# Nineteen gathered expert rows moved into the projections of tiles 1 to 3, in a layer kernel with product-key retrieval

## The chip, the cores and the metric

One Trainium2 chip, one of its cores. The metric is the device time of one execution in microseconds; the number given for a kernel is the median over its runs.

## What is computed

One layer over 512 positions (4 tiles of 128) and 2048 channels: a normed input projection, attention and a gated mix, an output projection added to `x`, and then the part that matters here, a retrieval of experts. Each position chooses 8 x 16 of 16384 experts by its query; each expert is one row of `peer_u` and one row of `peer_v` (2048 float32 numbers, 8 KB).

```python
def block(args):
    hb, idx, gb = args
    u_sel = jnp.take(expert_u, idx, axis=0)
    act = jax.nn.gelu(jnp.einsum('tkd,td->tk', u_sel, hb).astype(jnp.float32), approximate=False) * gb
    v_sel = jnp.take(expert_v, idx, axis=0)
    return jnp.einsum('tk,tkd->td', act.astype(hb.dtype), v_sel)
```

## The kernel before

**Two ways to the same sum.** For 304 of the positions of tiles 1 to 3 the kernel computes all experts densely on TensorE (PE): weights stream through a ring in pieces of 1 MB (128 x 2048 float32). For tile 0 (128 positions) and the last 80 positions it gathers the chosen rows: one "row" is an indirect DMA that brings one expert row to each of 128 partitions, so again 1 MB. VectorE (DVE) takes each row of `peer_u` times the normed input and sums it (line 1461, "u" rows), ScalarE (ACT) takes the GELU, and DVE adds each row of `peer_v`, weighted, to an accumulator of four PSUM banks called `acc` (lines 1472 and 1474, "v" rows). There are 128 u and 128 v rows for tile 0, then `out` (adds x and stores tile 0), `h` (loads the input of the last positions), 64 + 16 u rows and 64 + 16 v rows: 419 entries in `ROWS`, always in that order, each tied by `ROWS_AT` (line 121) to a piece during whose turn DVE takes it.

**A piece.** `load_upto` (line 480, the sync queue SP) loads piece n once PE has freed its place. ACT writes the high half `ring_hi` (`hi_upto`, line 735, instruction at 744); DVE (`lo_upto`, line 1180, instruction at 1188) or GpSimd (POOL, `make_lo`, line 655, instruction at 658) writes the low half `ring_lo`; PE waits for the low half and multiplies. The ring has three slots in the output projection of tiles 1 to 3 (pieces 112 to 127, `OUT_B`, PE line 1847) and the query projection (128 to 143, `QUERY_B`, PE line 2130), and four from piece 144 (`AHEAD`) on.

**The stages.** Pieces 112 to 127 run from 749 us, 128 to 143 from 897 us, the up stage with retrieval from 1048 us (pieces 144 to 215, PE lines 2145 to 2147), the down stage (216 to 283) from about 1600 us, and the last stage, up and down in turn (284 to 395), from about 2060 to 2840 us. In all but a few pieces of the projections DVE makes the low halves.

**The order of the work on DVE.** In the output projection DVE's loop (line 1591) makes for piece n the low halves up to n + 1, adds x after every fourth piece (`add_x1`), makes the low halves up to n + 2 (line 1597), and takes the rows of n. In the query projection (line 1614) it makes the low halves up to n + 2 (line 1617) and then takes the rows. From line 1626 it finishes the query sums, copies `h_far` (tile 0's normed input) into `acc` (line 1637), so that the place of `h_far` becomes row buffer 3, and begins the retrieval of tiles 1 to 3.

**The order of the work on POOL.** POOL issues the gathers in the order of `ROWS` (`gather`, line 677, the DMA at 695 or 703), each when the row that last used its buffer has been taken (`row_used`). In the projections it has nothing else to do. From piece 144 on it makes the low half of n and then issues the gathers whose buffers should be free (`gather_freed_before`, line 671). The first row in buffer 3 (`H_ROW`) waits for the copy of `h_far` (line 691). After `out` its buffer's next gather first stores tile 0 and waits for that store (lines 684 and 685).

**Row buffers.** 8 KB a partition each. `row_buffers` (line 175) takes of those allowed at a row's position the one free longest: 0 and 1 always, 4 up to piece 104, 2 from piece 112, 3 from piece 144. So the projections have three.

## Time and profile before

| what | us |
|---|---|
| median of 3 runs (least, most) | 2888.29 (2881.99, 2889.8) |
| the profiled execution, by itself | 2884.2 |
| its span, first to last instruction | 2882.5 |
| PE busy in the span | 2769.8 |
| granted TensorE clock, mean | 0.986 |

The profile is of one execution. Busy time of PE is modelled for the end of a matmul, so matmul counts per stretch are read beside it. "DMA share" is the mean busy share of the core's 16 DMA engines, and GB/s what they moved.

### The profile page before, as it was taken

The page shows a single profiled execution, that of the slowest core. Times are in us where ns is not written, and L with a number is a line of the kernel's source. Part 1 is how long each engine was busy: PE and PEld are TensorE (multiplying, and loading weights), DVE is VectorE, ACT ScalarE, POOL GpSimd, SP SyncE. Part 2 cuts the span into 40 slices and gives each one's busy share as a digit, 9 for nine tenths or more (in the row PEclk, how much of TensorE's full clock was granted, in tenths as well). Part 3 has the DMA queues.
Part 4 walks back from the last instruction along what each step waited for, and adds up shares of the span by engine and source line. Part 5 has one row for each costly group of instructions (what it writes and reads, how often), then busy time and mean ns, then how long its engine had stood idle before and what let it go on. Part 6 is the DMA issues. An engine that isn't in the chain of part 4 may idle for free.

```text
span 2882.5 us, 43296 instructions
## 1 busy us (share of the span) xinstructions
PE 2769.8 (96%) x17757; PEld 2612.8 (91%) x17757; DVE 2156.8 (75%) x2920; ACT 1256.1 (44%) x1692; POOL 1485.8 (52%) x657
## 2 busy tenths in 40 slices
PE   8899999988999999999999999998999999999998
PEld 6687778866788999999999999998999999999998
DVE  6856897767587778889997677776676777777786
ACT  7656632347424333337775333333333333333332
POOL 0100253322232348872223788887867776767762
PEclk9999999999999999999999999999999999999999
DMA  9747678974697969998999999999999999999996
GB/s 362 297 154 273 242 265 344 341 268 156 252 347 289 359 255 338 339 347 346 361 363 372 379 367 382 375 373 336 359 370 358 385 363 378 377 384 361 384 344 229
DMA packets 188846, 949.47 MB, mean 329 GB/s; under 512 B 17712, under 2 KB 77152, under 8 KB 78912
## 3 DMA queue, kind: packets, MB, share of 16 engines
q1 hardware_dynamic: 116064, 485.54, 45.1%
q0 software_dynamic: 60848, 440.59, 39.2%
q10 hardware_dynamic: 11808, 21.70, 2.1%
q8 instruction: 74, 1.21, 0.2%
q14 instruction: 52, 0.43, 0.0%
HBM read 906.46 MB, written 41.22 MB: 329 GB/s over the span
## 4 chain that ended last, share of the span: by engine, by line
PE 73%; DMA 9%; DVE 9%; ACT 5%; POOL 2%; issue 2%; SPq 0%; ACTq 0%; DVEq 0%; POOLq 0%
PE ps L1847 9%; PE ps L2147 9%; PE ps L2145 9%; PE ps L2146 9%; PE ps L2214 8%; PE ps L2216 8%; PE ps L2215 8%; PE ps L2130 5%; PE ps L1834 3%; DVE ring_lo L1188 3%; DMA rows<-peer_u_rows,idx_far 2%; PE ps L2188 2%; DMA g_in<-gelu_scratch 2%; POOL ring_lo L658 2%; DVE rows L1461 2%; ACT ring_hi L744 2%
## 5 line engine op out<-in xcount | busy, mean ns | idle before, releaser
L658 POOL TENSOR_TENSOR ring_lo<-ring_raw,ring_hi 128x2048 fp32r<-128x2048 f32 x203 | 942.2, 4642 | 527.7 <-ACT ring_hi L744 525.6
L744 ACT ACTIVATE ring_hi<-ring_raw 128x2048 fp32r<-128x2048 f32 x396 | 754.7, 1917 | 664.8 <-DMA ring_raw<-peer_u 233.5
L2214 PE MATMUL ps<-a_hi,ring_hi 128*128 128x304 f32 x2048 | 624.0, 305 | 19.9 <-POOL ring_lo L658 13.8
L2145 PE MATMUL ps<-bT_hi,ring_hi 128*128 128x304 f32 x2048 | 622.7, 304 | 9.8 <-POOL ring_lo L658 8.3
L2216 PE MATMUL ps<-a_hi,ring_lo 128*128 128x304 f32 x2048 | 620.0, 303 | 0.0
L2147 PE MATMUL ps<-bT_hi,ring_lo 128*128 128x304 f32 x2048 | 617.8, 302 | 0.0
L2215 PE MATMUL ps<-a_lo,ring_hi 128*128 128x304 f32 x2048 | 617.0, 301 | 0.0
L2146 PE MATMUL ps<-bT_lo,ring_hi 128*128 128x304 f32 x2048 | 615.7, 301 | 0.0
L1188 DVE TENSOR_TENSOR ring_lo<-ring_raw,ring_hi 128x2048 fp32r<-128x2048 f32 x197 | 460.6, 2355 | 129.8 <-ACT ring_hi L744 129.5
L695 POOL DMA_INDIRECT rows<-peer_u_rows,idx_far x128 | 206.0, 1609 | 452.8 <-DVE z_far L1461 398.0
L2214 PEld LDWEIGHTS ps<-a_hi,ring_hi 128*128 128x128 f32 x2048 | 386.2, 189 | 25.2 <-issue 17.9
L2145 PEld LDWEIGHTS ps<-bT_hi,ring_hi 128*128 128x128 f32 x2048 | 386.6, 189 | 10.9 <-issue 5.2
L2215 PEld LDWEIGHTS ps<-a_lo,ring_hi 128*128 128x128 f32 x2048 | 387.3, 189 | 0.5 <-issue 0.5
L2216 PEld LDWEIGHTS ps<-a_hi,ring_lo 128*128 128x128 f32 x2048 | 386.7, 189 | 0.0
L2146 PEld LDWEIGHTS ps<-bT_lo,ring_hi 128*128 128x128 f32 x2048 | 386.7, 189 | 0.0
L2147 PEld LDWEIGHTS ps<-bT_hi,ring_lo 128*128 128x128 f32 x2048 | 386.5, 189 | 0.0
L1736 DVE TENSOR_TENSOR yT<-ps,yT 128x304 f32<-128x304 f32 x496 | 222.1, 469 | 142.5 <-PE ps L2216 127.5
L1474 DVE SCALAR_TENSOR_TENSOR ps<-rows,a_far,ps 128x2048 f32<-128x2048 f32 x127 | 298.4, 2350 | 35.9 <-DMA rows<-peer_v_rows,idx_far 27.9
L1461 DVE CUSTOM_DVE_ANT_0 rows<-rows,h_far 128x2048 f32<-128x2048 f32 x116 | 280.7, 2436 | 52.3 <-DMA rows<-peer_u_rows,idx_far 52.1
L695 POOL DMA_INDIRECT rows<-peer_v_rows,idx_far x128 | 150.0, 1172 | 206.4 <-DVE ps L1474 191.1
L1461 DVE CUSTOM_DVE_ANT_0 rows<-rows,ps 128x2048 f32<-128x2048 f32 x92 | 208.9, 2280 | 20.6 <-DMA rows<-peer_u_rows,chosen 11.3
L1847 PE MATMUL ps<-ring_hi,bT_hi 128*128 128x512 f32 x660 | 187.6, 393 | 9.7 <-DVE ring_lo L1188 9.0
(328 smaller groups left out, 3759.8 us busy)
## 6 DMA issues: line engine op xcount, KB each, us to landing
ring_raw<-peer_u SPq DMA_DIRECT2D x128, 1024.0 KB
ring_raw<-peer_v SPq DMA_DIRECT2D x128, 1024.0 KB
...
```

The costliest lines, as they stand in the source:

```text
L658: pool.tensor_tensor(ring_lo[s][:], ring_raw[s][:], ring_hi[s][:].bitcast(F32), ALU.subtract)\
L695: pool.indirect_dma_start(out=dst[:], out_offset=None, in_=u_rows if kind == "u" else v_rows, in_offset=bass.IndirectOffsetOnAxis(ap=idx_f ...
L744: act.activation(ring_hi[place(n)][:], ring_raw[place(n)][:], ACT.Copy).then_inc(hi_ok[SLOT[n]], 1)
L1188: dve.tensor_tensor(ring_lo[s][:], ring_raw[s][:], ring_hi[s][:].bitcast(F32), ALU.subtract)\
L1461: dve.tensor_tensor_reduce(out=src, in0=src, in1=h_far[:] if r < FIRST_PSUM_ROW else acc, scale=1.0, scalar=0.0, op0=ALU.mult, op1=ALU.add ...
L1847: last = pe.matmul(ps[:, bank + t, :], w[:, k, t * P:(t + 1) * P], m[s][:, cols], start=first, stop=end)
L2145: pe.matmul(dst, hi[:, e], bT_hi[:, k, 0:NEAR], start=(k == 0), stop=False)
L2146: pe.matmul(dst, hi[:, e], bT_lo[:, k, 0:NEAR], start=False, stop=False)
L2147: last = pe.matmul(dst, lo[:, e], bT_hi[:, k, 0:NEAR], start=False, stop=(k == KD - 1))
L2214: pe.matmul(dst, hi[:, col], a_hi[:, par, e, :], start=(e == 0), stop=False)
L2215: pe.matmul(dst, hi[:, col], a_lo[:, par, e, :], start=False, stop=False)
L2216: last = pe.matmul(dst, lo[:, col], a_hi[:, par, e, :], start=False, stop=(e == GROUP - 1))
```

## The change

The projections get row buffer 4 back: at its old place for positions 113 to 129, and for positions 134 to 143 at a new place, `rows_5`, in what was `x1B` (its gathers wait for what used those places before: `turned[MIX_NORM_B]` and `h3_stored`; ACT's copy of the first query scores waits for the last row of the first span). `ROWS_AT` gives pieces 112 to 126 thirty-five rows instead of 26 (three at 115, 117, ... 125) and pieces 128 to 141 thirty-eight instead of 28 (three at 129, 131, 133 and 135 to 141). The last stage has 128 instead of 147; the stages between keep 81 and 75. So all 128 u rows of tile 0 and seven v rows lie before piece 144; these seven are summed in `early_acc` in SBUF, and the eighth reads `early_acc` and writes `acc`. The copy of `h_far` into `acc`, and POOL's wait for it, are gone; buffer 3's first gather waits for row 134, the seventh v row. On DVE low halves are now made up to n + 1 only before the rows of n. By the order of `ROWS`, `out` moves from piece 270 to 252.

```diff
--- before.py
+++ after.py
@@ -147,7 +147,7 @@
         ROWS_AT[n] = 1 if n % 4 == 2 else 2
     ROWS_AT[OUT_B - 1] += sum(ATTEND_ROWS)
     for n in range(OUT_B, AHEAD - 1):
-        ROWS_AT[n] = 0 if n == QUERY_B - 1 else 1 if n == QUERY_B - 2 or n % 4 == 3 and n < QUERY_B else 2
+        ROWS_AT[n] = 0 if n == QUERY_B - 1 else 1 if n == QUERY_B - 2 else 3 if n % 2 and n > OUT_B + 2 or n > QUERY_B + 7 else 2
     ROWS_AT[AHEAD - 2] = 0
     for t in range(3):
         for r in range(len(RETRIEVE_ROWS)):
@@ -167,15 +167,19 @@
 fill_rows()
 ROW_POS = [n for n in range(N_PIECES) for _ in range(ROWS_AT[n])]
 FIRST_PSUM_ROW = min(r for r in range(N_ROWS) if ROW_POS[r] >= AHEAD)
+assert ROWS[FIRST_PSUM_ROW][0] == "v" and ROWS[FIRST_PSUM_ROW][1] > 0
+assert ROW_POS[ROWS.index(("v", 0))] > QUERY_B + 1
 
 
 MID_BUF = 2
+SIDE_A, SIDE_B, SIDE_C = range(0, 105), range(OUT_B + 1, QUERY_B + 2), range(QUERY_B + 6, AHEAD)
+SIDE_AT = (*SIDE_A, *SIDE_B, *SIDE_C)
 
 
 def row_buffers():
     bufs, prev, last = [], [], {}
     for r in range(N_ROWS):
-        have = [0, 1] + ([4] if ROW_POS[r] <= 104 else []) + ([MID_BUF] if ROW_POS[r] >= OUT_B and ROWS[r][0] != "v3" else []) + \
+        have = [0, 1] + ([4] if ROW_POS[r] in SIDE_AT else []) + ([MID_BUF] if ROW_POS[r] >= OUT_B and ROWS[r][0] != "v3" else []) + \
                ([3] if ROW_POS[r] >= AHEAD else [])
         b = min(have, key=lambda b: last.get(b, -1))
         bufs.append(b)
@@ -188,7 +192,10 @@
 ROW_FULL = [sum(16 * {"h": HALVES, "h3": EIGHTHS}.get(ROWS[q][0], 1) for q in range(r + 1) if ROW_BUF[q] == ROW_BUF[r])
             for r in range(N_ROWS)]
 ROW_LAG = 3
-H_ROW = ROW_BUF.index(3)
+LAST_SIDE_A = max(r for r in range(N_ROWS) if ROW_BUF[r] == 4 and ROW_POS[r] in SIDE_A)
+FIRST_SIDE_B = min(r for r in range(N_ROWS) if ROW_BUF[r] == 4 and ROW_POS[r] in SIDE_B)
+LAST_SIDE_B = max(r for r in range(N_ROWS) if ROW_BUF[r] == 4 and ROW_POS[r] in SIDE_B)
+FIRST_SIDE_C = min(r for r in range(N_ROWS) if ROW_BUF[r] == 4 and ROW_POS[r] in SIDE_C)
 
 
 def gather_lag(n):
@@ -288,6 +295,12 @@
     g_quad = [at("g_quad_0", [P, 4 * GATED], F32, 150), at("g_quad_1", [P, 4 * GATED], F32, 195)]
     g_in = [at("g_in_0", [P, NEAR], F32, 188), at("g_in_1", [P, NEAR], F32, 190)]
     rows = [at(f"rows_{b}", [P, D], F32, kb) for b, kb in enumerate((164, 172, 156, 180, 148))]
+    early_acc = at("early_acc", [P, D], F32, 112)
+    side_c = at("rows_5", [P, D], F32, 124)
+
+    def row_home(r):
+        return side_c if ROW_BUF[r] == 4 and ROW_POS[r] in SIDE_C else rows[ROW_BUF[r]]
+
     acc_mid = rows[MID_BUF]
     x_end = [at(f"x_end_{t}", [P, D], F32, 48 + 8 * t) for t in range(4)]
     acc_out = at("acc_out", [P, D], F32, 80)
@@ -381,7 +394,7 @@
         topk, sm_sub, sm_exp = sem("topk_step"), sem("softmax_sub"), sem("softmax_exp")
         far_sel, h_far_made, x1_stored = sem("far_selected"), sem("h_far_made"), sem("x1_stored")
         copied = sem("copied_to_psum")
-        RQ_A, RQ_B, H_FAR, ACC_MID = 1, 2, 3, 4
+        RQ_A, RQ_B, ACC_MID = 1, 2, 3
 
         vb_made, mixed, gated = sem("vb_made"), sem("mixed"), sem("gated")
         qk_normed, qk_turned, qkT_out = sem("qk_normed"), sem("qk_turned"), sem("qkT_out")
@@ -677,7 +690,7 @@
             def gather(r):
                 kind, s = ROWS[r]
                 b, prev = ROW_BUF[r], ROW_PREV[r]
-                dst = rows[b]
+                dst = row_home(r)
                 if prev >= 0:
                     pool.wait_ge(row_used, prev + 1)
                     if ROWS[prev][0] == "out":
@@ -687,8 +700,10 @@
                     pool.wait_ge(pv_done, HEADS)
                 elif b == 4:
                     pool.wait_ge(x1_stored, 16)
-                if r == H_ROW:
-                    pool.wait_ge(copied, H_FAR)
+                if r == FIRST_SIDE_B:
+                    pool.wait_ge(turned[MIX_NORM_B], KD)
+                elif r == FIRST_SIDE_C:
+                    pool.wait_ge(h3_stored, 16)
                 if kind == "u" and s == P // 2:
                     pool.wait_ge(far_sel, 2)
                 if kind == "u" or kind == "v":
@@ -802,7 +817,7 @@
                 if part_ == U_PART and half == 0:
                     act.wait_ge(x1_stored, 16)
                     act.wait_ge(h_far_made, 1)
-                    act.wait_ge(row_used, 1 + max(r for r in range(N_ROWS) if ROW_BUF[r] == 4))
+                    act.wait_ge(row_used, LAST_SIDE_A + 1)
                 for t in range(TB):
                     between(t)
                     dst = projB[part_][:, t, half * BANK:(half + 1) * BANK]
@@ -1040,6 +1055,7 @@
                 act.wait_ge(s_done, SB + 2 * c + 1)
                 if c == 0:
                     act.wait_ge(h3_made, 1)
+                    act.wait_ge(row_used, LAST_SIDE_B + 1)
                 for t in range(TB):
                     act.activation(scoreB[t][:, 4 * c:4 * c + 4, :].rearrange("p a n -> p (a n)"), ps[:, t, :],
                                    ACT.Copy).then_inc(sb_out, 1)
@@ -1445,7 +1461,7 @@
             def one_row(r):
                 kind, s = ROWS[r]
                 b = ROW_BUF[r]
-                src = rows[b][:]
+                src = row_home(r)[:]
                 z, a, gate, count = {"2": (z2, a2, gate2, G2), "3": (z3, a3, gate3, G3)}.get(
                     kind[-1], (z_far, a_far, gate_far, P))
                 if kind in ("v", "v2", "v3") and s % U_BATCH == 0:
@@ -1458,20 +1474,21 @@
                 if kind in ("u", "u2", "u3"):
                     if kind != "u" and s == 0:
                         dve.wait_ge(row_used, r)
-                    dve.tensor_tensor_reduce(out=src, in0=src, in1=h_far[:] if r < FIRST_PSUM_ROW else acc, scale=1.0,
+                    dve.tensor_tensor_reduce(out=src, in0=src, in1=h_far[:] if kind == "u" else acc, scale=1.0,
                                              scalar=0.0, op0=ALU.mult, op1=ALU.add, accum_out=z[:, s:s + 1])\
                        .then_inc(row_used, 1)
                 elif kind in ("v", "v2", "v3"):
-                    if kind == "v" and s == 0:
-                        dve.wait_ge(qb_sq, 16)
                     dve.wait_ge(row_used, r)
                     if kind == "v3" and s == 0:
                         dve.tensor_copy(acc_mid[:], acc).then_inc(copied, 1)
                         dve.wait_ge(copied, ACC_MID)
                     if s == 0:
-                        dve.tensor_scalar(acc, src, a[:, 0:1], None, ALU.mult).then_inc(row_used, 1)
+                        first = early_acc[:] if kind == "v" else acc
+                        dve.tensor_scalar(first, src, a[:, 0:1], None, ALU.mult).then_inc(row_used, 1)
                     else:
-                        dve.scalar_tensor_tensor(out=acc, in0=src, scalar=a[:, s:s + 1], in1=acc, op0=ALU.mult,
+                        before = early_acc[:] if r <= FIRST_PSUM_ROW else acc
+                        after = early_acc[:] if r < FIRST_PSUM_ROW else acc
+                        dve.scalar_tensor_tensor(out=after, in0=src, scalar=a[:, s:s + 1], in1=before, op0=ALU.mult,
                                                  op1=ALU.add).then_inc(row_used, 1)
                 elif kind == "out":
                     dve.wait_ge(row_used, r)
@@ -1594,7 +1611,6 @@
                     wait_piece(dve, n - 1)
                     for t in range(TB):
                         add_x1((n - OUT_B) // 4 - 1, t)
-                lo_upto(min(n + 2, QUERY_B))
                 rows_step(ROWS_AT[n])
             for t in range(TB):
                 if t < TB - 1:
@@ -1614,7 +1630,7 @@
             for n in range(QUERY_B, AHEAD):
                 if n > QUERY_B and n % 4 == 0:
                     add_squares((n - QUERY_B) // 4 - 1)
-                lo_upto(min(n + 2, AHEAD - 1))
+                lo_upto(min(n + 1, AHEAD - 1))
                 if n == QUERY_B + 1:
                     dve.wait_ge(s_nf, 32)
                     dve.wait_ge(x1_stored, 32)
@@ -1634,8 +1650,6 @@
             dve.wait_ge(qb_sq, 16)
             dve.tensor_copy(rq_ps, rqB).then_inc(copied, 1)
             dve.wait_ge(copied, RQ_B)
-            dve.tensor_copy(acc, h_far[:]).then_inc(copied, 1)
-            dve.wait_ge(copied, H_FAR)
             dve.wait_ge(h3_stored, 16)
 
             def row_between(s):
```

## Rows read from the trace of the kernel before

**Rows 1.** The page: busy time of each engine, its share of the span, instructions.

```profile
PE 2769.8 (96%) x17757; PEld 2612.8 (91%) x17757; DVE 2156.8 (75%) x2920; ACT 1256.1 (44%) x1692; POOL 1485.8 (52%) x657
```

**Rows 2.** Windows by stage: length, busy (count) per engine, PEclk, DMA share, GB/s.

```profile
749.00:872.00 123.00, 123.00 (x546) 101.88 (x545) 92.43 (x75) 35.21 (x35) 44.02 (x24) 1.00 0.84 319
897.00:1034.00 137.00, 137.00 (x833) 137.00 (x833) 103.49 (x82) 49.42 (x57) 43.60 (x26) 1.00 0.79 304
1100.00:1300.00 200.00, 200.00 (x1456) 200.00 (x1455) 168.84 (x512) 80.63 (x77) 162.53 (x60) 1.00 0.95 343
1600.00:1900.00 300.00, 296.27 (x2107) 294.85 (x2108) 220.63 (x312) 117.09 (x136) 251.97 (x95) 0.99 0.99 374
2060.00:2840.00 780.00, 771.22 (x5554) 769.08 (x5553) 568.54 (x615) 269.26 (x237) 565.92 (x244) 1.00 0.95 369
```

**Rows 3.** Windows of 10 us: the starts of two stages, and the change to retrieval.

```profile
750.00:760.00 10.00, 10.00 (x46) 8.27 (x45) 7.33 (x6) 1.80 (x1) 3.02 (x2) 1.00 0.14 43
900.00:910.00 10.00, 10.00 (x59) 10.00 (x59) 8.92 (x6) 2.11 (x2) 2.69 (x1) 1.00 0.26 89
1050.00:1060.00 10.00, 6.20 (x38) 5.95 (x36) 9.88 (x52) 3.84 (x4) 7.85 (x5) 0.84 0.84 306
1060.00:1070.00 10.00, 9.46 (x51) 9.46 (x52) 9.92 (x54) 0.10 (x1) 9.84 (x4) 0.71 0.71 292
1070.00:1080.00 10.00, 10.00 (x75) 10.00 (x74) 9.90 (x41) 4.59 (x4) 6.92 (x4) 1.00 0.86 292
```

**Rows 4.** PE timeline, 1040 to 1105 us: start, duration, instruction, idle before and releaser.

```profile
1060.54 0.62 PE L2145 MATMUL ps<-bT_hi,ring_hi 128*128 128x304 f32 x1 [4.34 <-POOL ring_lo L658]
```

**Rows 5.** POOL timeline, 1030 to 1070 us.

```profile
1032.68 4.61 POOL L658 TENSOR_TENSOR ring_lo<-ring_raw,ring_hi 128x2048 fp32r<-128x2048 f32 x1 [11.07 <-ACT ring_hi L744]
1051.22 0.96 POOL L695 DMA_INDIRECT rows<-peer_u_rows,idx_far  x1 [13.93 <-DVE ps L1637]
...
1055.95 13.64 POOL L658 TENSOR_TENSOR ring_lo<-ring_raw,ring_hi 128x2048 fp32r<-128x2048 f32 x3
```

**Rows 6.** DVE timeline, 750 to 1051 us.

```profile
754.11 2.29 DVE L1461 CUSTOM_DVE_ANT_0 rows<-rows,h_far 128x2048 f32<-128x2048 f32 x1
...
756.32 2.29 DVE L1461 CUSTOM_DVE_ANT_0 rows<-rows,h_far 128x2048 f32<-128x2048 f32 x1
...
1032.04 0.08 DVE L1461 DVE_READ_ACCUMULATOR2_ANT z_far<- 128x1 f32 x1
...
1048.15 2.29 DVE L1637 COPY ps<-h_far 128x2048 f32<-128x2048 f32 x1
```

**Rows 7.** Windows of 20 us with idle PE in the last two stages.

```profile
2000.00:2020.00 20.00, 14.53 (x85) 14.54 (x86) 7.90 (x12) 4.11 (x5) 17.43 (x7) 0.74 0.86 336
2160.00:2180.00 20.00, 18.08 (x131) 17.84 (x130) 12.73 (x16) 8.29 (x6) 13.61 (x6) 1.00 0.79 302
2760.00:2780.00 20.00, 16.96 (x119) 16.22 (x117) 18.92 (x13) 5.08 (x6) 11.49 (x6) 1.00 0.87 325
```

**Rows 8.** PE timeline, 749 to 783 us: first matmuls of pieces 113 and 116.

```profile
757.41 0.84 PE L1847 MATMUL ps<-ring_hi,bT_hi 128*128 128x512 f32 x3
...
781.89 0.84 PE L1847 MATMUL ps<-ring_hi,bT_hi 128*128 128x512 f32 x3
```

**Rows 9.** DVE by source line: ns least/median/most of the two weighted-sum forms.

```profile
L1474 DVE SCALAR_TENSOR_TENSOR ps<-rows,a_far,ps x127: 2343/2348/2357, 1147.8 to 1969.0; 128x2048 f32<-128x2048 f32 x127
...
L1622 DVE SCALAR_TENSOR_TENSOR x1B<-x1B,small,nfB x1: 2347/2347/2347, 915.2 to 915.2; 128x2048 f32<-128x2048 f32 x1
```

**Rows 10.** Waits, 1970 to 2025 us: who waited for whom, us, times, longest.

```profile
POOL rows L703 <- DMA y<-rows: 7.8, 1, 7.8
```

**Rows 11.** ACT timeline, 745 to 885 us: the high half of piece 118.

```profile
792.98 1.92 ACT L744 ACTIVATE ring_hi<-ring_raw 128x2048 fp32r<-128x2048 f32 x1 [1.61 <-DMA ring_raw<-w_out]
```

**Rows 12.** POOL timeline, 745 to 885 us: two gathers of the output projection.

```profile
756.67 2.75 POOL L695 DMA_INDIRECT rows<-peer_u_rows,idx_far  x1 [21.77 <-DVE z_far L1461]
759.73 0.94 POOL L695 DMA_INDIRECT rows<-peer_u_rows,idx_far  x1 [0.30 <-issue]
```

## The prediction

> **What bounds the kernel.** First the page's line of busy times: PE is busy in 2769.8 of 2882.5 us [rows 1]. What other engines save counts only where PE stands still, and PE's 112.7 idle us are the most that could be had. Next the windows by stage. In the last stage, which gives up 19 rows, PE is busy in 771.2 of 780 us: the DMA engines are full (share 0.95), but PE hides nearly all of it. In the two projections, which receive them, PE is never idle: 123.0 of 123 and 137.0 of 137 us. There the DMA share is 0.84 and 0.79 and DVE is busy 92.4 and 103.5 us [rows 2]. So the change moves work from a stage where it costs little to one where nothing is lost today. The third thing to see is the end of the query projection: 89 matmuls run from 1050 to 1070 us where 75 per 10 us follow, at a clock of 0.84 and 0.71 of 2.4 GHz [rows 3].
>
> **Part 1, the copy of h_far and the wait for it.** PE waits 4.34 us for a low half from POOL at 1056 us, the longest stall near this edit [rows 4]. POOL had made one low half by 1037.3 and then stood for 13.9 us behind a gather that waits for the copy; three low halves follow only from 1055.95 [rows 5]. The copy starts at 1048.15, when all query sums are done, while DVE took its last u row by 1032.1 [rows 6]. After the change that gather waits for row 134, of piece 141. Taken on time, at about 1034, it lets POOL issue four gathers (under 5 us by the spacing of rows 5) and finish the next low half before 1047. The stall goes, and with it the half clock behind it: 150 - 89 = 61 matmuls were lost in the 20 us; at 200 us / 1456 = 0.137 us each [rows 2, 3] that is 8.4 us. Part of the slow clock may come from PE's short waits during the last query sums, just before, and those stay; I take 7. Bounds: 0 if row 134 comes later than 1046, 8.4 at best. DVE also begins retrieval 2.3 us earlier; PE is full from 1100 to 1300 us [rows 2], so that is worth 0.
>
> **Part 2, the rows taken from the last stage.** 19 x 1.05 MB at its 369 GB/s are 54 us of DMA time, and 19 x 2.35 = 45 us of DVE time (for 2.35 see part 3). Neither is on the path: PE idles 780 - 771.2 = 8.8 us there [rows 2], and that is the bound. Of these, 1.9 us lie in a window in which the DMA share dips to 0.79, as where a load is late, and 3.0 us in the one where the sum is copied ahead of the last sixteen v rows [rows 7], which costs DVE 18.9 of 20 us whatever the number of rows. I take 4; bounds 0 and 8.8.
>
> **Part 3, the rows put into the projections: DVE.** Two u rows start 2.21 us apart, so that is the price of one row [rows 6]. Nine more up to the time at which PE starts piece 127 make 92.4 + 19.9 = 112.3 of 123 us; ten more make 103.5 + 22.1 = 125.6 of 137 us. DVE fits as a whole. It does not fit piece by piece: a piece of the output projection takes (781.89 - 757.41) / 3 = 8.16 us [rows 8], and three rows and one low half 4 x 2.21 = 8.8 us. From piece 135 to 141 there are seven such pieces in a row. The seven v rows read and write SBUF, which no row of `v` shows; with PSUM the form takes 2348 ns, and the nearest one in SBUF alone, at line 1622, 2347 ns [rows 9]. So 0, with bounds of 0.1 us to either side.
>
> **Part 4, the same rows: DMA.** The projections moved 319 x 123 = 39.2 MB (thousands of GB/s x us) and 304 x 137 = 41.6 MB. Per unit of share that is 319 / 0.84 = 380 and 304 / 0.79 = 385 GB/s, and 369 / 0.95 = 388 in the last stage [rows 2]; this is what the engines carry here when full. With nine and ten rows of 1.049 MB they have 48.7 and 52.1 MB to move: 48.7 / 0.380 = 128 us against 123, and 52.1 / 0.385 = 135 against 137. Both stages begin with a gap, since all buffers are full then and no row is taken: shares of 0.14 and 0.26 in 10 us [rows 3]. Some of it remains, because buffer 4's first gather waits for the end of the norm's turn (about 749 us) with the others queued behind it on POOL; rows behind the first low half instead of the second make it shorter. I put 2 us on each stage. That is 7 us late in the first and 0 in the second; the buffers let rows run about one piece late before a low half is late, which takes back some, and in the second stage the seven full pieces stand at its end and give some. I take 6 + 3 = 9 us of PE idle; bounds 0 (the lag fits into the ring's slack) and 24 (rival B).
>
> The Trainium skill ("DMA: Bandwidth & Descriptors", section "Where 436 GB/s comes from") gives about 358 GB/s as what HBM lets one core have and says that this binds between HBM and SBUF. By it, as an estimate, the two stages would need 136 and 145 us and lose 21 us. The trace contradicts it: 374 GB/s over 300 us and 369 over 780 us [rows 2].
>
> **Part 5, the order on DVE, the added waits and `out`.** A low half n + 1 ahead of the rows of n comes one group of rows later than n + 2 did, but DVE itself runs a piece ahead, having less to wait for; 0 on its own, and without that lead the 6.6 us of three rows would stand ahead of a low half. ACT's wait for row 100 comes when DVE is at piece 132, three pieces later: 0. If late, it would hold `ring_hi` behind it. POOL's wait for `h3_stored` is ahead of row 112, at piece 134, and the store starts near piece 130: 0; only gathers are queued behind it. `out` costs a POOL wait of 7.8 us for its store [rows 10], in which no low half is made; PE misses 61 of 146 matmuls in the 20 us from 2000 us [rows 7]. Moved 18 pieces ahead it meets the same queue: 0, with bounds of -8 (it falls into slack) and +3.
>
> **Sum.** -7 - 4 + 9 + 0 = -2 us: 2884.2 - 2 = 2882 us beside this execution. The median of the runs is 4.1 us above it, so I predict 2886. The measurement tells about 0.3%, 8.7 us, from no change: 2879.6 to 2897.0 is "same".
>
> **Rival A, faster: the projections take the rows for nothing.** The DMA gaps at both starts close, four buffers bridge the pairs of full pieces, and PE stays full. For it: before, PE has no idle at all with DVE at 75% and DMA at 0.84, and in the retrieval stage it has none at a share of 0.95 [rows 2]. Against it: 0.95 there goes with one row a piece and four ring slots. Price: -7 - 4 - 2 (part of the `out` wait) = -13: 2875 us. Chance 0.33.
>
> **Rival B, slower: the piece load becomes late behind four gathers.** In a ring of three slots a load may start when PE ends piece n - 3 and must have been halved twice before piece n: two pieces, 16.3 us. High and low half take 1.92 + 2.29, so a load has 12.1 us. One took until 792.98, that is 11.1 us after its slot came free at 781.89 [rows 8, 11], with three buffers. Four gathers and one load are 5.24 MB, at 385 GB/s 13.6 us: 1.5 us late. It decides from the point where four gathers are under way as a load begins. There are 6 pieces with three rows in the output projection and 10 in the query projection (its pieces, 48 matmuls at 59 in 10 us [rows 3], are as long), so it costs 16 x 1.5 = 24 us: -11 + 24 = +13, 2901 us. POOL adds to it: a gather takes 2.75 instead of 0.94 us while DVE is at work [rows 12], and three at 3.05 us are 9.2 us, over a piece. Against it: DVE's pace spaces the gathers, and a late PE gives time back. Chance 0.23.
>
> **Rival C: the first gather of the up stage waits as before.** If the v rows of piece 141 are as late as 1046 us, `row_used` takes the place of the copy and the 7 us are not won: -4 + 9 = +5, 2893 us. It needs 12 us of lateness that PE does not share, which the low half of 143, behind those rows, hardly lets happen. Chance 0.05.
>
> **Rival D: the projections carry less than 380 GB/s.** The retrieval stage moves 343 GB/s at a share of 0.95, 361 at 1 [rows 2]. If the added gathers bring the projections to that, they need 48.7 / 0.361 = 135 and 52.1 / 0.361 = 144 us, 19 too many with the gaps at the starts filled: -11 + 19 = +8, 2896 us. The skill's figure in part 4 would act like this. Against it are the two stretches near 370 and the projections' own 380 at a share of 1. Chance 0.05.
>
> **Chances.** Forecast 0.34, A 0.33, B 0.23, C 0.05, D 0.05. A reaches 2871 if all 8.8 us of the last stage come back; B's middle is 2901. The range 2871 to 2903 leaves out half of B's upper part and a little of A. Faster by over 0.3%: nearly all of A and the lower edge of the forecast, 0.35. Within: the rest of the forecast, C, half of D, a little of B, 0.42. Slower: 0.23. The forecast's own range is 2879 to 2894.
>
> **What would show it.** Part 1: no PE wait for POOL near 1056 us, and 73 to 75 matmuls per 10 us after the first few. Part 2: PE busy over 775 of 780 us in the last stage, DMA share near 0.9. Parts 3 and 4: DMA share over 0.95 and DVE over 90% in both projections, and PE waits for `ring_lo` from line 1188 of some 9 us, most of them behind pieces 119 to 125 and 138 to 142. Were PE still at 100% there, parts 3 and 4 are wrong and A is right; PE waits on many pieces with gathers landing after 13 us speak for B. A stage between them that changes by more than 3 us would be something I have not seen.

## The result and the profile after

The changed kernel takes 2892.68 us (median of 20 runs, 2883.3 to 2905.07); the kernel before, timed beside it, 2882.31 (20 runs). The ratio is 1.0038 [1.0027, 1.0049]: 0.38% slower, some 11 us, where I had forecast 2 us less. The profiled execution took 2899.75 us by itself, with a span of 2898.0 against 2882.5: 15.5 us to be explained. That execution is 7 us above the median of its twenty. Each kernel of this document was profiled in one execution, so the length of a stage below is that of one execution, while whole kernels are compared by all their runs. The page's busy times answer to [rows 1]:

```profile
PE 2773.7 (96%) x17757; PEld 2614.1 (90%) x17757; DVE 2202.7 (76%) x2919; ACT 1255.2 (43%) x1692; POOL 1508.0 (52%) x657
```

PE does the same 17757 matmuls and is busy 3.9 us longer; the other 11.6 us are idle. The next thing to read is where. From the PE timeline of both kernels I took the first matmul of each stage; the differences add up to the span's:

| stage (us) | before | after | difference | forecast |
|---|---|---|---|---|
| up to the output projection | 749.1 | 744.7 | -4.4 | 0 |
| output projection | 148.5 | 154.8 | +6.3 | +6 |
| query projection | 150.2 | 164.9 | +14.7 | +3 |
| up stage | 562.5 | 553.7 | -8.8 | -7 |
| down stage | 471.4 | 464.2 | -7.2 | 0 |
| last stage, to its last up matmul | 746.5 | 760.6 | +14.1 | -4 |
| what follows | 54.3 | 55.1 | +0.8 | 0 |

The start varies between 739 and 750 us over all profiles of this study, also of kernels with nothing changed ahead of it, and the down stage between 464 and 479. The five kernels below that are nearest to this one have 471 to 478 there, so I read nothing into those two rows. The two large errors are the query projection and the last stage, which was given 19 rows less and became longer. Windows of the kernel after (length, busy and count per engine, PEclk, DMA share, GB/s), answering to [rows 2, 3]:

```profile
744.00:870.00 126.00, 121.37 (x527) 98.53 (x526) 110.52 (x93) 33.69 (x35) 72.18 (x34) 0.99 0.96 390
899.00:1055.00 156.00, 145.88 (x858) 144.60 (x857) 125.01 (x96) 50.45 (x60) 70.11 (x37) 0.97 0.85 333
1070.00:1080.00 10.00, 10.00 (x75) 10.00 (x74) 9.96 (x29) 7.28 (x7) 7.82 (x2) 1.00 0.62 202
1618.00:2082.00 464.00, 457.40 (x3262) 455.67 (x3263) 341.08 (x516) 181.71 (x205) 388.30 (x146) 1.00 1.00 374
2082.00:2843.00 761.00, 745.76 (x5330) 742.62 (x5329) 542.20 (x535) 254.26 (x224) 521.18 (x216) 0.99 0.92 338
...
800.00:810.00 10.00, 9.79 (x44) 7.74 (x43) 9.34 (x9) 1.92 (x1) 7.15 (x4) 1.00 1.01 424
850.00:860.00 10.00, 7.65 (x32) 5.88 (x31) 8.59 (x9) 2.30 (x7) 5.66 (x3) 0.92 1.01 421
1020.00:1030.00 10.00, 5.88 (x32) 5.56 (x31) 7.71 (x8) 1.91 (x1) 1.96 (x2) 0.96 1.01 427
```

In the last stage DMA fell from 369 to 338 GB/s, yet PE idles 15.2 us, twice as long. In the output projection the DMA engines carry 390 GB/s, and over 420 at full share, more than the 380 that I had taken as full. Who held PE, in the projections (PE waits of the output projection, then of the query projection: total, times, longest):

```profile
PE ps L1861 <- DVE ring_lo L1204: 4.6, 4, 2.4
...
PE ps L2144 <- DVE ring_lo L1204: 10.1, 4, 5.0
```

These stops stand against growths of 6.3 and 14.7 us. The next term is the clock, which fell to half for a while behind the longest stops: as a mean of 10 us it is 0.83 of 2.4 GHz from 854 to 864 us, 0.74 and 0.92 from 939 to 959, and 0.83 from 1029 to 1039. Worked out from these windows, PE lost 1.7 us by it in the output projection and 5.1 in the query projection.

**The last stage.** ACT waits less for loads than before (waits, 2060 to 2840 us before, and 2075 to 2855 after), so high halves are ready earlier. But one kind of DVE instruction, with the same shapes and nearly the same count, costs 37 us more (groups of instructions, same stretches: busy us, mean ns). First the kernel before, then after:

```profile
ACT ring_hi L744 <- DMA ring_raw<-peer_u: 187.5, 52, 10.6
ACT ring_hi L744 <- DMA ring_raw<-peer_v: 88.3, 36, 7.1
...
L1188 DVE TENSOR_TENSOR ring_lo<-ring_raw,ring_hi 128x2048 fp32r<-128x2048 f32 x29 | 75.3, 2597 | 0.0
```

```profile
ACT ring_hi L759 <- DMA ring_raw<-peer_u: 118.5, 51, 4.9
ACT ring_hi L759 <- DMA ring_raw<-peer_v: 36.3, 18, 8.0
...
L1204 DVE TENSOR_TENSOR ring_lo<-ring_raw,ring_hi 128x2048 fp32r<-128x2048 f32 x28 | 112.6, 4022 | 0.0
```

A mean hides what happens; the timeline shows it. First DVE and POOL of the kernel before, where POOL's low half begins after DVE's has ended; then of the kernel after, where they begin together; the last line is PE's:

```profile
2230.70 2.28 DVE L1188 TENSOR_TENSOR ring_lo<-ring_raw,ring_hi 128x2048 fp32r<-128x2048 f32 x1
2234.89 4.63 POOL L658 TENSOR_TENSOR ring_lo<-ring_raw,ring_hi 128x2048 fp32r<-128x2048 f32 x1 [3.72 <-ACT ring_hi L744]
```

```profile
2176.65 6.93 DVE L1204 TENSOR_TENSOR ring_lo<-ring_raw,ring_hi 128x2048 fp32r<-128x2048 f32 x1
2176.82 4.61 POOL L671 TENSOR_TENSOR ring_lo<-ring_raw,ring_hi 128x2048 fp32r<-128x2048 f32 x1
...
2204.38 2.28 DVE L1204 TENSOR_TENSOR ring_lo<-ring_raw,ring_hi 128x2048 fp32r<-128x2048 f32 x1
2204.47 6.65 POOL L671 TENSOR_TENSOR ring_lo<-ring_raw,ring_hi 128x2048 fp32r<-128x2048 f32 x1 [1.46 <-ACT ring_hi L759]
...
2230.97 6.48 DVE L1204 TENSOR_TENSOR ring_lo<-ring_raw,ring_hi 128x2048 fp32r<-128x2048 f32 x1
2230.68 4.62 POOL L671 TENSOR_TENSOR ring_lo<-ring_raw,ring_hi 128x2048 fp32r<-128x2048 f32 x1 [1.08 <-ACT ring_hi L759]
...
2183.71 0.40 PE L2228 MATMUL ps<-a_hi,ring_hi 128*128 128x304 f32 x1 [1.57 <-DVE ring_lo L1204]
```

When both halves, each reading two SBUF tiles, start within 0.3 us, one keeps its duration and the other lasts about the sum: 2.28 + 4.61 = 6.89 against 6.93 for DVE, or 6.65 for POOL at 2204 us. So the two exclude one another here. Eleven of DVE's 28 low halves are such long ones (6.4 to 7.1 us), against one or two before. PE's waits in the last stage of the kernel after (total, times, longest):

```profile
PE ps L2228 <- DVE ring_lo L1204: 9.6, 11, 1.9
...
PE ps L2228 <- DVE a_lo L1689: 3.2, 2, 2.7
PE ps L2228 <- POOL ring_lo L671: 2.8, 1, 2.8
PE ps L2228 <- DVE yT L1750: 2.2, 1, 2.2
```

Eleven waits for DVE's low half stand where there was one, of 2.2 us. PE idles 15.2 us in the stage against 7.1 before (746.5 less 739.4 busy). That is 8.1 of the 14.1; the other 6 are longer busy time for the same matmuls, and the clock accounts for 5 of them. It fell to half for some us (0.83 to 0.84 of 2.4 GHz as a mean of 10 us) right after the three longest stops, of 2.8 (POOL), 1.9 (DVE's low half) and 2.7 us (`a_lo`), and after none of this kernel's shorter ones in the stage. Windows of 10 us with them, matmul counts first in brackets, where 74 are normal:

```profile
2282.00:2292.00 10.00, 10.00 (x63) 10.00 (x63) 6.57 (x7) 2.03 (x3) 9.51 (x5) 0.84 0.86 297
2562.00:2572.00 10.00, 8.12 (x48) 7.88 (x48) 9.47 (x6) 1.48 (x3) 4.80 (x2) 0.83 0.86 355
2762.00:2772.00 10.00, 7.29 (x42) 7.04 (x41) 8.95 (x9) 4.03 (x3) 6.05 (x3) 0.83 0.61 215
```

The length of a stop does not decide this by itself. The kernel before has stops of 1.9 and 2.15 us at 2170 and 2774 us with the clock at 1.00 [rows 7], and two of 1.88 us in d4 below were not followed by a slow clock either; why is open.

So PE waited less for each meeting than DVE lost in it (4.6 us), since DVE runs ahead; what weighs is the sum of many small stops and the clock after the few long ones.

### The profile page after: what moved, and what is told of

It is laid out like the page before. It is cut to its first block, busy times and chain, and to the rows that moved or that the text cites. A ratio compares the mean times of both kernels' runs of the same rounds, so it can differ in the third digit from the quotient of the medians.

```text
span 2898.0 us, 43282 instructions
## 1 busy us (share of the span) xinstructions
PE 2773.7 (96%) x17757; PEld 2614.1 (90%) x17757; DVE 2202.7 (76%) x2919; ACT 1255.2 (43%) x1692; POOL 1508.0 (52%) x657
## 4 chain that ended last, share of the span: by engine, by line
PE 66%; DVE 13%; DMA 11%; ACT 6%; POOL 2%; issue 2%; SPq 0%; DVEq 0%; ACTq 0%; POOLq 0%
PE ps L2228 8%; PE ps L2230 8%; PE ps L2229 8%; PE ps L2161 8%; PE ps L2159 8%; PE ps L2160 8%; PE ps L1861 8%; DVE ring_lo L1204 6%; DMA rows<-peer_u_rows,idx_far 5%; DVE rows L1477 3%; PE ps L1848 3%; ACT ring_hi L759 2%; PE ps L2202 2%; DMA ring_raw<-peer_u 2%; PE ps L2144 2%
## 5 line engine op out<-in xcount | busy, mean ns | idle before, releaser
L671 POOL TENSOR_TENSOR ring_lo<-ring_raw,ring_hi 128x2048 fp32r<-128x2048 f32 x203 | 951.9, 4690 | 502.4 <-ACT ring_hi L759 501.1
L1204 DVE TENSOR_TENSOR ring_lo<-ring_raw,ring_hi 128x2048 fp32r<-128x2048 f32 x197 | 500.5, 2557 | 97.3 <-ACT ring_hi L759 96.8
L710 POOL DMA_INDIRECT rows<-peer_u_rows,idx_far x128 | 231.3, 1807 | 390.6 <-DVE z_far L1477 334.2
L1477 DVE CUSTOM_DVE_ANT_0 rows<-rows,h_far 128x2048 f32<-128x2048 f32 x128 | 307.0, 2416 | 60.1 <-DMA rows<-peer_u_rows,idx_far 59.9
L1491 DVE SCALAR_TENSOR_TENSOR ps<-rows,a_far,ps 128x2048 f32<-128x2048 f32 x120 | 282.1, 2351 | 31.6 <-DMA rows<-peer_v_rows,idx_far 26.4
L1861 PE MATMUL ps<-ring_hi,bT_hi 128*128 128x512 f32 x660 | 188.7, 395 | 11.3 <-DVE ring_lo L1204 10.6
L1861 PE MATMUL ps<-ring_hi,bT_lo 128*128 128x512 f32 x660 | 186.6, 391 | 0.0
## 6 DMA issues: line engine op xcount, KB each, us to landing
gelu_scratch<-ahead ACTq DMA_DIRECT2D x72, 152.0 KB
g_in<-gelu_scratch SPq DMA_DIRECT2D x72, 152.0 KB
```

The lines of the kernel that those rows point to most:

```text
L671: pool.tensor_tensor(ring_lo[s][:], ring_raw[s][:], ring_hi[s][:].bitcast(F32), ALU.subtract)\
L710: pool.indirect_dma_start(out=dst[:], out_offset=None, in_=u_rows if kind == "u" else v_rows, in_offset=bass.IndirectOffsetOnAxis(ap=idx_f ...
L1204: dve.tensor_tensor(ring_lo[s][:], ring_raw[s][:], ring_hi[s][:].bitcast(F32), ALU.subtract)\
L1477: dve.tensor_tensor_reduce(out=src, in0=src, in1=h_far[:] if kind == "u" else acc, scale=1.0, scalar=0.0, op0=ALU.mult, op1=ALU.add, accum ...
L1861: last = pe.matmul(ps[:, bank + t, :], w[:, k, t * P:(t + 1) * P], m[s][:, cols], start=first, stop=end)
```

## The experiments

**Last stage: four kernels.** All low halves of the last stage on POOL, in the kernel after (a1) and in the kernel before (a4):

```diff
-        return (n - BOTH) % 2 == 0 or (n - BOTH) // 2 % 2 == 0
+        return True
```

> The changed kernel, but in the last stage POOL makes every low half of the ring, also the one in four that DVE made. Theory L (in the last stage the low halves of DVE and POOL now fall together, and each such meeting holds DVE for 4.4 us: 11 of 28 in the changed kernel's profile, 1 of 27 in that of before): with DVE's low halves gone no meeting is possible, PE waits in the last stage fall from 9.6 us for DVE's low halves to about 0, the stage shortens by 5 to 9 us, and the kernel comes to 0.9965 to 1.001 of before. Theory P (all of the loss is in the two projections, and the last stage is late by chance of one run): the stage stays within 2 us and the ratio stays 1.003 to 1.005. POOL would be busy some 5.8 of 6.6 us a piece; if that is too much, PE waits for POOL's low half appear and the kernel is slower than the changed one.

> The kernel before with all low halves of the last stage on POOL: the control for the first run. Theory L: before had 1 meeting of 27, so little is to be had: within 4 us of before, and a gain well under that of the first run against the changed kernel. If DVE's load and not the meetings is what counts, it gains as much as the first run does. If POOL becomes too full with 147 rows (5.9 of 6.6 us a piece), it is slower.

The kernel before without the last nineteen `v2` rows, which leaves out part of the sum, and nothing else (a2); and the kernel before with buffer 3 from piece 152 instead of 144, which takes the gather that waits for the copy of `h_far` out of the way and leaves the copy (a3):

```diff
-        [("v2", s) for s in range(G2)] + [("v3"
+        [("v2", s) for s in range(G2 - 19)] + [("v3"
```

```diff
-               ([3] if ROW_POS[r] >= AHEAD else [])
+               ([3] if ROW_POS[r] >= AHEAD + 8 else [])
```

> The kernel before without 19 of the weighted rows of the last 80 positions, all in the last stage (so 128 rows there, as in the changed kernel, and nothing added elsewhere); that part of the sum is left out. The prediction's part 2: 4 us faster, 0 to 8.8, PE idle in the last stage under 5 us. Theory L: the loads come earlier, POOL's low halves start with DVE's, several of DVE's low halves take 6.4 to 7.1 us instead of 2.3, PE idle in the last stage rises to about 15 us, and the kernel is 2 to 8 us slower than before although it does less. Theory P: 0 to 5 us faster.

> The kernel before with row buffer 3 allowed from piece 152 on instead of 144: the first gathers of the up stage no longer stand behind the copy of h_far, and nothing else changes. The prediction's part 1: 7 us faster (0 to 8.4), no PE wait of 4.3 us for POOL near 1056 us and 73 to 75 matmuls per 10 us after the first few. Rival: something else holds the low half at that point (the load of the next piece), and it is within 2 us of before.

| kernel | us | ratio to before (2881.18) | last stage | long low halves on DVE |
|---|---|---|---|---|
| a1, after + POOL | 2881.89 | 1.0010 [0.9999, 1.0022] | 737.9 | none in the stage |
| a2, before - 19 rows | 2892.38 | 1.0041 [1.0028, 1.0054] | 753.4 | 10 |
| a3, before, buffer 3 late | 2871.12 | 0.9964 [0.9947, 0.9980] | 743.1 | 0 |
| a4, before + POOL | 2877.16 | 0.9984 [0.9969, 0.9998] | 741.8 | none in the stage |

a2 is the plainest: a kernel that does less, with nothing added, is 0.41% slower. The loss of the last stage is not paid for rows put elsewhere; taking rows out is enough. The size was missed: 2 to 8 us had been expected, and the ratio says 12, of which the profile has 6.9 in the stage. a1 shows the cure, and that the gain was there to be had: PE is then busy in all but 0.1 us of the stage, by the window of a1.

```profile
2085.00:2823.00 738.00, 737.89 (x5328) 737.43 (x5327) 433.40 (x508) 254.90 (x224) 640.23 (x245) 1.00 0.94 348
```

That is 22.7 us less than after and 8.6 less than before, in one execution each. By all the runs a1 is 0.28% below the kernel after, some 8 us. a3 confirms part 1 by itself: the up stage is 552.9 us, 9.6 less, with no buffer, row or order changed in the projections.

**Is it the lighter DMA or DVE's shorter work that makes them meet?** In the kernel before, 19 rows of the last stage, every seventh, were made light: 16 columns instead of 2048, on DVE (d3), in the gather (d4), or both (d2). Part of the sum is left out or wrong by that. The cut shows the v rows on DVE; u rows are made light in the same way. The light gather is a plain load of 8 KB, which takes POOL 0.59 us to issue instead of 0.96.

```diff
+                    if r in LIGHT:
+                        pool.dma_start(dst[:, 0:16], v_rows[0:P, 0:16]).then_inc(gathered[b], 16)
+                        return
...
+                    elif r in LIGHT:
+                        dve.scalar_tensor_tensor(out=acc[:, 0:16], in0=src[:, 0:16], scalar=a[:, s:s + 1],
+                                                 in1=acc[:, 0:16], op0=ALU.mult, op1=ALU.add).then_inc(row_used, 1)
```

> The kernel before; in the last stage 19 of the 147 rows, one in seven, are gathered and multiplied in 16 of 2048 columns only (that part of the sum is left out). As with 19 rows left out: 8 to 12 of DVE's 28 low halves take 6.4 to 7.1 us, last stage 751 to 758 us. If the other placing of the rows and not their weight made the meetings, there are 0 to 2 and the stage is 740 to 746 us.

> The same 19 rows gathered in full, but multiplied in 16 columns only. If DVE's shorter work brings the low halves together: as many meetings as with both light. If the earlier loads do: 0 to 2 meetings, last stage 740 to 746 us.

> The same 19 rows gathered in 16 columns only, but multiplied in full (with stale data in the other columns, so that the sum is not the reference's). If the earlier loads bring the low halves together: 8 to 12 meetings, last stage 751 to 758 us. If DVE's shorter work does: 0 to 2, and 740 to 746 us.

| kernel | us | ratio to before (2882.26) | last stage | long low halves |
|---|---|---|---|---|
| d2, both light | 2881.23 | 1.0001 [0.9989, 1.0014] | 745.7 | 6 |
| d3, DVE light | 2879.78 | 0.9996 [0.9979, 1.0013] | 745.2 | 2 |
| d4, gather light | 2887.31 | 1.0020 [1.0003, 1.0038] | 747.6 | 9 |

The meetings come with the lighter DMA, not with DVE's shorter rows. But in these profiles the stage did not grow as a2's did: the 751 to 758 us expected of d2 and d4 were missed. d4's profile is of a short execution, 2877.32 us against a median of 2887.31, so its stage may be longer in most of the others; the kernel as a whole is 0.20% slower. d2's profile is near its median, and its six meetings cost nothing that shows. PE's waits of d4's profile:

```profile
PE ps L2220 <- DVE ring_lo L1194: 6.8, 8, 1.9
PE ps L2220 <- DVE a_lo L1681: 0.8, 1, 0.8
```

Waits for DVE's low half are 6.8 us where before had 2.2, and the other waits of before (POOL 3.7, `yT` 1.7, `a_lo` 1.2) are nearly gone: in this execution the relief of the DMA pays for the meetings. In a2 and in the kernel after, two waits for `a_lo` of 3.5 and 3.2 us in all come on top, one of 2.7 us in each. The DVE timeline of the kernel after shows another meeting ahead of it, of an instruction so small that I had not looked at it (DVE, DVE, then POOL and PE):

```profile
2752.55 2.28 DVE L1204 TENSOR_TENSOR ring_lo<-ring_raw,ring_hi 128x2048 fp32r<-128x2048 f32 x1
2754.75 4.57 DVE L1471 TENSOR_TENSOR a<-a,chosen 128x16 f32<-128x16 f32 x1
...
2752.87 6.41 POOL L671 TENSOR_TENSOR ring_lo<-ring_raw,ring_hi 128x2048 fp32r<-128x2048 f32 x1 [0.17 <-ACT ring_hi L759]
...
2765.45 0.41 PE L2228 MATMUL ps<-a_hi,ring_hi 128*128 128x304 f32 x1 [2.71 <-DVE a_lo L1689]
```

The weights' product of 16 columns, 0.2 us of work, takes 4.57 us: it ends as POOL's low half ends, at 2759.3. Behind it stand a copy, a v row and what `a_lo` waits for. In d4 the same product took 0.23 us, and the long wait for `a_lo` is missing. But this does not explain the lengths of the stage. The kernel before has the slow product too, with 4.55 us at 2752.94, and waits 1.2 us in all for `a_lo`; in e1 below it took 0.16 us, and the stage is as long as 757.6 us. Why eight to eleven meetings go with 753 to 761 us in some kernels (a2, b3, e1, after) and with 748 and 749 in others (d4, d1) stays open.

**The projections, one part at a time**, all on the kernel before: buffer 4 with its waits, rows as before (b1); with the order n + 1 too (b2); with that and the nine rows of the output projection (b3); or the ten of the query projection (b4).

```diff
-                lo_upto(min(n + 2, QUERY_B))
...
-                lo_upto(min(n + 2, AHEAD - 1))
+                lo_upto(min(n + 1, AHEAD - 1))
```

> The kernel before with only the fourth row buffer in the projections (its two places and its waits), the rows where they were. Theory Q (a fourth gather under way makes the ring's loads late, rival B of the prediction): the output and the query projection grow from 148.5 and 150.2 us by 2 us or more each, with the same rows. Theory R (it is the number of rows, three in a piece, that DVE and the DMA engines can't take; the buffer by itself is harmless): both stay within 1 us. Whole kernel within 5 us of before by R, 4 to 10 us slower by Q.

> The fourth buffer and DVE's new order (low halves up to n + 1 only ahead of the rows of n), the rows where they were. The prediction's part 5 has 0 for the order: both projections within 1 us of the run with the buffer alone. If the order costs, PE waits for DVE's low halves appear in the projections though no row was added.

> Fourth buffer, new order and nine more rows in the output projection alone (35; 28 in the query projection; 138 in the last stage; the copy of h_far stays). Theory R: output projection about 154 to 156 us as in the changed kernel, query projection 150 to 152. Forecast's price for it: +6.

> Fourth buffer, new order and ten more rows in the query projection alone (38; 26 in the output projection; 137 in the last stage; the copy of h_far stays). Theory R: output projection 148 to 149 us, query projection 162 to 166 us as in the changed kernel. If it stays under 158, the late rows of the output projection have a part in the changed kernel's 164.9. Forecast's price for it: +3.

| kernel | us | ratio to before (2884.21) | output / query projection | last stage, long |
|---|---|---|---|---|
| b1, buffer | 2881.37 | 0.9980 [0.9962, 0.9998] | 144.9 / 150.1 | 749.2, 2 |
| b2, buffer, order | 2881.82 | 0.9997 [0.9981, 1.0013] | 144.7 / 150.1 | 745.4, 0 |
| b3, + 9 rows | 2893.84 | 1.0034 [1.0011, 1.0058] | 153.5 / 150.0 | 755.3, 8 |
| b4, + 10 rows | 2889.52 | 1.0025 [1.0010, 1.0040] | 146.8 / 165.9 | 750.1, 4 |

Buffer and order cost nothing while the rows are few. The buffer even makes the output projection 3.6 us shorter, where at most 1 us had been expected; without it that stage takes 147.0 to 150.1 us in all profiles with 26 rows. The rows do cost, each in its own projection: nine are 8.8 us in the output projection (153.5 against 144.7), and ten 15.8 in the query projection. The kernel after has both at once (154.8 and 164.9). b3 and b4 have 138 and 137 rows in the last stage, and meetings there too.

**DVE's ten operations or the DMA's ten transfers?** Both on the kernel before with the order n + 1, in the ten pieces that get a row in the query projection: one more DVE product of two SBUF tiles in each (c1), or one more plain 1 MB load in each, from POOL (c2). Neither has the rows themselves.

```diff
+                for _ in range(DUMMY_AT.get(n, 0)):
+                    dve.tensor_tensor(spare[:], h_far[:], h_far[:], ALU.mult).then_inc(s_xa, 1)
...
+                pool.dma_start(spare[j % 2][:], v_rows[128 * j:128 * (j + 1), :]).then_inc(spare_in[j % 2], 16)
```

> The kernel before with DVE's new order and, in the query projection, ten products of two SBUF tiles on DVE that nothing reads (2.2 us each, as a row has), behind the rows of pieces 131, 133 to 141; no gather is added. If DVE's time is what the query projection lacks, it grows from 150.1 to some 160 to 166 us, as with ten more rows (165.9). If the DMA engines are, it stays under 153.

> The kernel before with DVE's new order and, in the query projection, ten loads of 1 MB on POOL's queue that nothing reads, one ahead of the first gather of each of the same ten pieces; DVE does nothing more. If the DMA engines are what it lacks (the prediction's part 4), the query projection grows from 150.1 to some 160 to 166 us and the ring's loads become late; if DVE is, it stays under 153. If both grow by a part only, it takes the two together.

One run each: the query projection takes 151.0 us with c1 and 157.6 with c2 (the whole 2882.55 and 2891.67), against 150.1 without and 165.9 with both in the form of rows (b4, which has buffer 4 too). DVE alone costs 0.9 us and the loads 7.5, which lies between the two values that had been expected of c2. Ten rows cost 15.8, so 7.4 us come only with both; no run has both without being rows. The trace of the kernel after shows it at 946 us (timeline: ACT, two rows and a low half of DVE, PE):

```profile
934.90 1.92 ACT L759 ACTIVATE ring_hi<-ring_raw 128x2048 fp32r<-128x2048 f32 x1 [2.98 <-DMA ring_raw<-w_query]
...
935.58 2.29 DVE L1477 CUSTOM_DVE_ANT_0 rows<-rows,h_far 128x2048 f32<-128x2048 f32 x1 [2.13 <-DMA rows<-peer_u_rows,idx_far]
940.90 2.29 DVE L1477 CUSTOM_DVE_ANT_0 rows<-rows,h_far 128x2048 f32<-128x2048 f32 x1 [3.02 <-DMA rows<-peer_u_rows,idx_far]
...
944.06 2.29 DVE L1204 TENSOR_TENSOR ring_lo<-ring_raw,ring_hi 128x2048 fp32r<-128x2048 f32 x1
...
946.40 0.69 PE L2144 MATMUL ps<-bT_hi,ring_hi 128*128 128x384 f32 x1 [4.98 <-DVE ring_lo L1204]
```

The high half was ready at 934.90 + 1.92 = 936.8, and DVE turned to it at 944.06, 7.2 us later, because two rows stood ahead of it and the second was late. So PE waits for work whose data have long been there.

**The length of the run of full pieces, and the order.** c3 is the kernel after with pieces 136, 138, 140 back at two rows and 137, 139 and 141 too (six rows fewer there, 134 in the last stage). d1 is the kernel after with the low half n + 2 ahead of the rows again in both projections, e1 in the query projection alone, and e2 is e1 with all low halves of the last stage on POOL.

```diff
-        ... else 3 if n % 2 and n > OUT_B + 2 or n > QUERY_B + 7 else 2
+        ... else 3 if n % 2 and OUT_B + 2 < n < QUERY_B + 8 else 2
```

> The changed kernel with six rows fewer at the end of the query projection (pieces 136 to 141 have two again; 32 rows there instead of 38), so 134 in the last stage. If the run of seven pieces with three rows is what costs, the query projection falls from 164.9 to 150 to 154 us, and, the last stage being between the meetings of 128 and 138 rows (753 to 758 us), the kernel is at 0.996 to 1.000 of before.

> The changed kernel with DVE's old order (low halves up to n + 2 ahead of the rows of n). If the new order is what costs when rows are late (at 946 us PE waited 5.0 us for a low half whose high half had been ready at 936.8, while DVE waited for a row), the two projections fall from 154.8 and 164.9 us to some 150 and 156. If the loads themselves are late, or the rows' number decides, they stay or grow: the old order has DVE wait for the load of n + 2 with rows lying ready, and the output projection comes to 155 to 160 us.

> The kernel after, with the low half n + 2 ahead of the rows of n again, in the query projection alone; the output projection keeps n + 1. In the kernel after, PE stands 4.98 and 4.12 us for low halves whose high halves had been ready for 7 and 10 us, since DVE stood in rows. If that order is what costs the query projection, it falls from 164.9 to 150 to 156 us, the output projection stays at 152 to 155, and the whole is 6 to 12 us shorter than the kernel after, so within 0.3% of the kernel before. If it was the output projection's own lateness that made the query projection short in the kernel with both orders undone (154.2), the query projection stays above 160 us.

> The same, and all low halves of the last stage on POOL. By the theory that both losses are separate and both cured, output 152 to 155, query 150 to 156, up stage near 553, last stage 738 us: 7 to 14 us below the kernel before, ratio 0.995 to 0.998, and no better than the kernel before with buffer 3 late and the low halves on POOL (0.9948). If the last stage takes the rows back as stalls, its length is over 742 us.

The kernel before took 2882.6 us beside c3, 2882.26 beside d1, and 2884.24 beside e1 and e2.

| kernel | us | ratio to before | output / query | up | last, long |
|---|---|---|---|---|---|
| c3 | 2894.68 | 1.0043 [1.0025, 1.0060] | 152.0 / 158.4 | 555.6 | 744.0, 3 |
| d1 | 2894.97 | 1.0047 [1.0019, 1.0075] | 167.4 / 154.2 | 552.1 | 749.3, 8 |
| e1 | 2889.66 | 1.0011 [0.9990, 1.0031] | 153.5 / 154.9 | 554.1 | 757.6, 11 |
| e2 | 2873.16 | 0.9967 [0.9948, 0.9985] | 153.0 / 155.0 | 552.5 | 737.3, none in the stage |

c3 missed what was expected of it, 150 to 154 us in the query projection and 0.996 to 1.000 in all: the stall at 946 us is still there, 5.13 us long, and it lies ahead of the run of seven full pieces. Why c3's runs are no shorter than those of the kernel after, while its profiled stages are, stays open. e1 decides the question of the order: one line turned back brings the query projection from 164.9 to 154.9 us, so with these rows in it, 10 of its 14.7 us go with the order and 4.7 stay; without them the order cost nothing (b2). In the output projection the same line works the other way, 154.8 with n + 1 and 167.4 with n + 2, where 150, or 155 to 160, had been expected of d1. So the change helped in the one and hurt in the other. e2 shows that the losses are separate: with the order turned back and the meetings gone, the 19 moved rows are in a kernel 0.33% faster than before, though the query projection still takes 155.0 us.

**Without the move at all.** c4 is the kernel before with buffer 3 late (a3) and the low halves of the last stage on POOL (a4), both edits above.

> The kernel before with row buffer 3 from piece 152 on and all low halves of the last stage on POOL: the two edits that each gained, and no row moved. If they add: 0.9955 to 0.993 of before, last stage near 738 us and up stage near 553 us. If the time taken from one is given back in the other, 0.996 to 0.998.

It takes 2867.42 us, 0.9948 [0.9929, 0.9967], the lowest ratio of this study, though its interval overlaps that of a3 alone: up stage 552.4, last stage 738.3 us. Its window of the last stage:

```profile
2071.00:2810.00 739.00, 738.36 (x5332) 738.08 (x5331) 478.22 (x546) 256.45 (x224) 656.58 (x263) 1.00 0.98 374
```

All 147 rows are there, at a DMA share of 0.98, and PE is full. So moving rows out was not needed: the stage is 8.2 us shorter than before with every row in it. I had read the share of 0.95 as the bound of that stage.

**Are the meetings what POOL's taking over removes, or DVE's load?** In each of four pairs it takes 28 low halves of 2.28 us, 64 us of work, off DVE in the last stage. With all 147 rows, and so with hardly a meeting, that makes the stage 4.7 us shorter (before, a4) and 4.8 (a3, c4). With 128 rows and eleven meetings it is 22.7 (after, a1) and 20.3 (e1, e2). If the load alone counted, the four would be alike, so some 16 to 18 us of these profiles are the meetings and the stops and slow clock behind them. All the runs point the same way with more noise: 0.16% and 0.16% against 0.28% and 0.44%.

## Why the prediction was wrong, by its steps

The measured 2892.68 us lie inside my range of 2871 to 2903, but the kernel became slower and not 2 us faster. The range held because rival B's price stood in it, so for another cause than the one that acted; that is luck. The steps that failed are parts 2 and 5.

**Part 1 was right.** The wait of 4.34 us for POOL near the start of the up stage is gone, 75 matmuls per 10 us follow (the window at 1070 above), and the stage is 8.8 us shorter where I said 7; a3 gives 9.6 for that step alone. Rival C falls.

**Part 2 failed, in sign.** "I take 4; bounds 0 and 8.8" left out that a stage can lose when its DMA is relieved. I had excluded a loss without a reason for it; I had never asked which instruction comes earlier when loads come earlier, and what it then meets. The step showed +14.1. That the 8.8 us of idle PE could be had is right: a1 gets 8.6 of them. The trace before had the number. Of the 3.0 us at 2760 us [rows 7], which I put down to the copy ahead of the last sixteen v rows, 2.15 were a wait for one of DVE's low halves, held by POOL's (DVE, POOL and PE of the kernel before):

```profile
2767.26 6.93 DVE L1188 TENSOR_TENSOR ring_lo<-ring_raw,ring_hi 128x2048 fp32r<-128x2048 f32 x1
2767.43 4.61 POOL L658 TENSOR_TENSOR ring_lo<-ring_raw,ring_hi 128x2048 fp32r<-128x2048 f32 x1
2774.33 0.40 PE L2214 MATMUL ps<-a_hi,ring_hi 128*128 128x304 f32 x1 [2.15 <-DVE ring_lo L1188]
```

The way to it was the group's mean: 2597 ns stands above the 2290 of the same instruction in the query projection, and a mean that differs between two stages for the same shape was the row to follow. The Trainium skill ("SBUF — State Buffer", section "Who interferes with whom") says that a DVE instruction with two SBUF inputs contends with a GpSimd instruction that reads SBUF, and that the order of issue decides which one blocks. The trace agrees that one waits until the other has ended, with 6.93 us for a held DVE and 6.65 for a held POOL. It does not show what decides: the recorded starts have DVE 0.17 us ahead where it is held (2176 us) and 0.09 us ahead where POOL is (2204 us).

**Part 3 was right as a sum** (c1: 0.9 us for ten more operations). It missed one operation: the eighth v row reads `rows` and `early_acc`, both in SBUF, and took 6.61 us at 1072 us beside a low half of POOL, where the six ahead of it took 2.35; PE did not stop for it.

**Part 4 came out in the output projection** (+6.3 against 6), **in good part by luck.** I worked out 380 GB/s as rate over share; the engines carried 390 over 126 us and up to 427 in 10 us, so "this is what the engines carry here when full" is refuted. A shortage there was all the same, over a shorter stretch. From 774 to 864 us the share is 0.99 to 1.01 in each 10 us, at 416 GB/s on average. Pieces 115 to 125 need 28 rows and 11 loads, 40.9 MB, and at that rate 98 us, where PE needs 11 x 8.16 = 90 (an estimate from these windows and [rows 8]). That is near the 8.8 us by which nine rows lengthen the stage in b3. The sum came to 6 because three errors made up for each other: too low a rate, taken over the whole stage; the buffer, which gives 3.6 us back and had no number; and the 1.7 us of slow clock, which had no term. In the query projection the share is 0.85 over the stage, so nothing is short as a whole; there I read the lateness as bunching. The stage begins with ten us in which nothing moves (a share of 0.01, in the kernel before too), and the next forty run at 0.96 to 1.00, up to the stall (windows of after):

```profile
899.00:909.00 10.00, 10.00 (x62) 10.00 (x61) 8.65 (x10) 4.84 (x5) 1.99 (x1) 1.00 0.01 2
909.00:919.00 10.00, 10.00 (x60) 10.00 (x59) 10.00 (x7) 1.92 (x1) 5.43 (x3) 1.00 0.96 344
...
939.00:949.00 10.00, 5.02 (x22) 4.70 (x22) 8.10 (x8) 1.91 (x1) 1.29 (x3) 0.74 1.00 409
```

I had that gap in the sum, at 2 us. No run here closed it, so this stays a reading.

**Part 5 failed, and it is the term that was mis-sized in the query projection.** "0 on its own, and without that lead the 6.6 us of three rows would stand ahead of a low half": the condition was named and its case priced at nothing. Without DVE's lead, since rows were late, low halves stood 7.2 us behind rows, and the query projection lost 10 us to it (e1). The sum should have carried that as a case with its own chance, tied to part 4: late rows and the order are one mechanism. The sum also counted PE's idle time alone; the 5.1 us at half clock behind the stops of this stage had no term in it. Of the rest of part 5, the wait for the store of `out` is there as before (7.7 us against 7.8) and PE idles 6.5 us in the down stage against 10.6, but that stage varies too much for a reading. With the case of late rows and with part 2's sign known, the parts come to -8.8 + 6.3 + 14.7 + 14.1 = +26 us in the profiled execution, less the 11.6 of start and down stage, which vary by themselves; +0.8 for the end gives 15.5.

**Rivals.** A is out, since PE stood still in both projections. B put a loss in the right place and nearly of the right size (24 us against 21) for another cause: it made the loads late, while at the longest stall, 946 us, the high half was there and DVE was not. D is refuted by the 390 GB/s. The slower case that decided as much as B, two engines meeting in a stage that had been relieved, was not among them. I had written that a change of over 3 us in a stage between would be new to me; it was the stage at the end that was.
